# Scale half of the first modulation loaded ahead of the shift half, the low-rank shift added in PSUM, decay midpoints as the exponential's bias

## The reference

```python
sh1, sc1, ... = mod                       # mod = silu(cond) @ ada_w + ada_b, 6 x 1024 columns
h = rms_norm(x, pre_mix_g) * (1.0 + sc1) + sh1
proj = h @ w_in                           # conv value and gate, r, k, v
w_raw = w0 + tanh(h @ w1) @ w2            # decay, for each of two directions
w_log = -softplus(-w_raw) - 0.5
decay = exp(-exp(w_log))
a = sigmoid(a0 + (h @ a1) @ a2)
g = sigmoid(h @ g1) @ g2
```

## Time and profile before

| | us |
|---|---|
| median of 3 runs (lowest to highest) | 1207.55 (1206.76 to 1209.17) |
| the profiled execution's own time | 1206.84 |
| its span | 1205.0 |
| TensorE busy | 1123.2 (93%) |
| VectorE busy | 393.8 (33%) |
| ScalarE busy | 199.2 (17%) |

### The profile page before, as it was taken

One profiled execution on the slowest core, in us unless ns is written; L12 is line 12 of the kernel. 1 busy time (PEld: TensorE's weight loads), 2 busy tenths in 40 slices (PEclk: granted clock), 3 DMA queues, 4 the chain that ended last, 5 costly groups with the idle time before them and its releaser, 6 DMA issues.

```text
span 1205.0 us, 16442 instructions
## 1 busy us (share of the span) xinstructions
PE 1123.2 (93%) x6676; PEld 510.6 (42%) x6676; DVE 393.8 (33%) x935; ACT 199.2 (17%) x458; POOL 68.1 (6%) x113
## 2 busy tenths in 40 slices
PE   4999999999999999898999999999999898989997
PEld 2886776744434333333333333344333333333432
DVE  0598887654321212121212121213212121212123
ACT  2311344423111110101010101011111111110102
POOL 1003444400000000000000000000000000000000
PEclk9999999999999999999999999999999999999999
DMA  9900746888999999999999999999999999999995
GB/s 369 386 29 10 311 174 247 311 308 327 423 413 432 432 432 427 430 429 430 431 431 430 431 430 431 419 424 432 431 431 430 431 432 430 430 432 424 427 425 243
DMA packets 39948, 456.11 MB, mean 379 GB/s; under 512 B 5168, under 2 KB 5696, under 8 KB 16352
## 3 DMA queue, kind: packets, MB, share of 16 engines
q1 hardware_dynamic: 39112, 454.58, 90.0%
q0 software_dynamic: 480, 0.80, 0.2%
q10 hardware_dynamic: 312, 0.11, 0.0%
HBM read 454.13 MB, written 1.34 MB: 378 GB/s over the span
## 4 chain that ended last, share of the span: by engine, by line
PE 50%; DMA 44%; DVE 4%; issue 1%; ACT 1%; SPq 0%; DVEq 0%; ACTq 0%
DMA ring<-in_w_gu 39%; PE bank L637 24%; PE bank L675 5%; PE bank L757 5%; DMA front<-in_w_down 3%; DMA ring<-in_ada_w 2%; PE bank L1028 2%; PE bank L592 2%; PE bank L582 1%; PE bank L752 1%; PE bank L872 1%; PE bank L767 1%; PE bank L814 1%; PE bank L887 1%; PE bank L617 1%
## 5 line engine op out<-in xcount | busy, mean ns | idle before, releaser
L637 PE MATMUL bank<-ring,front 128*64 128x512 f32 x2032 | 461.3, 609 | 36.0 <-DMA ring<-in_w_gu 36.0
L637 PEld LDWEIGHTS bank<-ring,front 128*64 128x64 f32 x2032 | 143.9, 140 | 351.2 <-issue 283.8
L1521 DVE TENSOR_SCALAR front<-bank 128x512 f32<-128x512 f32 x32 | 22.1, 692 | 481.6 <-PE bank L637 481.6
L675 PE MATMUL bank<-front 128*64 128x512 f32 x512 | 113.6, 595 | 9.5 <-ACT front L1159 9.1
L675 PE MATMUL bank<-ring,front 128*64 128x512 f32 x512 | 113.4, 595 | 5.1 <-ACT front L1159 5.1
L1151 ACT ACTIVATE front<-front 128x512 f32<-128x512 f32 x32 | 20.2, 631 | 488.1 <-DVE front L1521 488.1
L1545 DVE COPY front<-bank 64x512 f32<-64x512 f32 x32 | 21.9, 683 | 175.1 <-PE bank L675 175.1
L675 PEld LDWEIGHTS bank<-front 128*64 128x64 f32 x512 | 36.3, 137 | 76.5 <-issue 73.3
L675 PEld LDWEIGHTS bank<-ring,front 128*64 128x64 f32 x512 | 36.3, 137 | 71.9 <-issue 70.4
L592 PE MATMUL bank<-front 128*128 128x512 f32 x136 | 62.9, 605 | 1.5 <-DVE front L1545 1.5
L582 PE MATMUL bank<-front 128*128 128x128 f32 x480 | 56.0, 275 | 0.0
(11 more groups left out here) (272 smaller groups left out, 901.6 us busy)
## 6 DMA issues: line engine op xcount, KB each, us to landing
ring<-in_w_gu SPq DMA_DIRECT2D x46, 4096.0 KB
front<-in_w_down SPq DMA_DIRECT2D x30, 2048.0 KB, 19.5
ring<-in_w_down SPq DMA_DIRECT2D x28, 2048.0 KB, 20.2
ring<-in_w_gu SPq DMA_DIRECT2D x25, 2048.0 KB
ring<-in_ada_w SPq DMA_DIRECT2D x24, 1024.0 KB, 11.7
ring<-in_w_gu SPq DMA_DIRECT2D x20, 1024.0 KB
ring<-in_w_in SPq DMA_DIRECT2D x5, 2048.0 KB, 19.9
ring<-in_w_down SPq DMA_DIRECT2D x6, 1024.0 KB, 10.1
```

The costliest lines, as they stand in the source:

```text
L637: last = pe.matmul(ps[r][64 * hf:64 * hf + 64, :], xT[:, k, S * q:S * q + S], rows, start=False, stop=(k == order[-1]))
L675: last = pe.matmul(ps[2][64 * c:64 * c + 64, :], actT[:, m, 64 * hf:64 * hf + 64], wdn[q][hf][:, m, c * 512:(c + 1) * 512], start=(k == 0) ...
L1521: v.tensor_scalar(glu, ps[0], 7.0, None, ALU.min).then_inc(s["glu_ready"], 1)
```

## The change

- The scale columns of `ada_w` are loaded first, in eight pieces of 512 KB; then `lora1`; then the shift columns, in four pieces of 1 MB that cover two k each. Their four semaphores are ones used later for something else, whose later waits are raised by 16.
- TensorE's order is: scale products of k = 0 to 3 (four column tiles of 256 columns now), the eight small transposes, k = 4 and 5, the transposes of x, k = 6 and 7, two turned blocks. ScalarE and VectorE write `hT` without the shift, and TensorE runs the first two low-rank products on it.
- Then, for each k, TensorE runs the four shift matmuls and one matmul of the third low-rank product. The shift is turned (two blocks) and lands in `shift_pad` (32 columns per k, two used, cleared by POOL). `shift_pad` times `lora1` (eight matmuls of 384 columns, four column tiles) is copied to `shift_l1`, and three matmuls against a 0/1 pattern add it to the three banks.
- `hT` is written again with scale and shift while this goes on; the projections wait for it, and items 4 to 7 wait because their banks hold x. The decay products wait for two `mids` in place of three.
- The third block of `w_in` waits for 16 counts of `ada0_acc` in place of 8.
- The sums in `Pc` keep their origin. VectorE writes plus and minus half of KAPPA times their last columns to `mid_log` (two small operations per q in place of eight), and ScalarE takes eight exponentials of 129 columns per head pair in place of two of 516, with `mid_log` as bias.

The core of the diff:

```diff
             for k in range(KC):
-                sp.dma_start(ada0[:, k, :], ada_w[k * P:(k + 1) * P, 0:2048]).then_inc(in_ada0[k], 16)
+                sp.dma_start(ada0[:, k, D:2 * D], ada_w[k * P:(k + 1) * P, D:2 * D]).then_inc(in_ada0[k], 16)
             for hf in range(2):
                 sp.dma_start(lora1[:, 4 * hf:4 * hf + 4, :], lora1_in[:, 4 * hf:4 * hf + 4, :])\
                     .then_inc(s["in_lora_b" if hf else "in_lora"], 16)
+            for k in range(0, KC, 2):
+                sp.dma_start(ada0[:, k:k + 2, 0:D], ada_w[k * P:(k + 2) * P, 0:D].rearrange("(k p) n -> p k n", p=P))\
+                    .then_inc(in_shift[k // 2], 16)
...
-                    sp.wait_ge(s["ada0_acc"], KC)
+                    sp.wait_ge(s["ada0_acc"], 2 * KC)
...
+            def first_rows_of(k, col):
+
+                for j in range(4):
+                    last = pe.matmul(ps[0][32 * j:32 * j + 32, 0:256], siluT[:, k, :],
+                                     ada0[:, k, col + j * 256:col + j * 256 + 256],
+                                     start=(k == 0), stop=(k == KC - 1), skip_group_check=True)
+                last.then_inc(s["ada0_acc"], 1)
...
+            pe.wait_ge(s["silu"], 1)
+            scale_rows(range(4))
...
+            scale_rows(range(4, 6))
             pe.wait_ge(s["xn"], 2)
...
+            scale_rows(range(6, KC))
             keep_clock(1)
             pe.wait_ge(s["mod0"], 1)
+            turn_first(0)
             keep_clock(1)
             for k in range(KC):
...
                 for n in range(2):
+                    pe.matmul(bank_of(n)[:, 0:N], lora1[:, k, n * P:(n + 1) * P], hT[:, k, :],
+                              start=(k == 0), stop=False, skip_group_check=True)
+            for k in range(KC):
+                if k % 2 == 0:
+                    pe.wait_ge(in_shift[k // 2], 16)
+                first_rows_of(k, 0)
+                pe.matmul(bank_of(2)[:, 0:N], lora1[:, k, 2 * P:3 * P], hT[:, k, :], start=(k == 0), stop=False,
+                          skip_group_check=True)
+            pe.wait_ge(s["mod0"], 2)
+            turn_first(256)
+            pe.wait_ge(s["modT"], 2)
+            for k in range(KC):
+                j = k % 4
+                last = pe.matmul(ps[0][32 * j:32 * j + 32, 0:3 * P], shift_pad[:, k, :], lora1[:, k, :],
+                                 start=(k < 4), stop=(k >= 4), skip_group_check=True)
+            last.then_inc(s["mod0_tr"], 1)
+            pe.wait_ge(s["in_rw"], 32)
+            pe.wait_ge(s["mod0"], 3)
+            for n in range(3):
+                pe.matmul(bank_of(n)[:, 0:N].rearrange("p (g t) -> p g t", g=G), shift_l1[:, n * P:(n + 1) * P],
+                          const[:, K_E2:K_E2 + G].unsqueeze(2).broadcast_to([P, G, T]), start=False, stop=True,
+                          skip_group_check=True).then_inc(s["l2_mm"], 1)
...
+                if 4 <= n < 8:
+
+                    rewritten = s["hT_a"] if n < 6 else s["hT_v"]
+                    pe.wait_ge(rewritten, KC + 4 * (n % 2 + 1))
...
-                    pe.wait_ge(s["a_sig"], 3)
+                    pe.wait_ge(s["a_sig"], 2)
...
                 for sg, sc in enumerate((-KAPPA, KAPPA)):
-                    last = a.activation(Ex[:, sg], Pc[:, :, r], ACT.Exp, scale=sc)
+                    for d in range(2):
+                        for g in range(G):
+                            last = a.activation(Ex[:, sg, d, g, :], Pc[:, d, r, g, :], ACT.Exp, scale=sc,
+                                                bias=mid_log[:, sg, r, d, g:g + 1])
...
+            po.memset(shift_pad, 0.0)
             po.memset(siluT, 0.0).then_inc(s["silu_pad"], 1)
...
+            v.wait_ge(s["ada0_acc"], 2 * KC)
+            v.tensor_copy(mod0[:, 256:512], ps[0][:, 0:256]).then_inc(s["mod0"], 1)
+            v.wait_ge(s["mod0_tr"], 2)
+            for m in range(2):
+                last = v.tensor_tensor(shift_pad[:, :, 0:G].rearrange("p (f h l) r -> p l f h r", f=2, h=2)[:, m], turned(m),
+                                       by_half(first_T[:, 0], m, 0), ALU.add)
+            last.then_inc(s["modT"], 1)
+            v.wait_ge(s["modT"], 2)
+            for c in range(KC):
+                hf, m = divmod(c, 4)
+                v.tensor_scalar(hT[:, c, T:N], ps[3 + c // 4][:, (c % 4) * T:(c % 4 + 1) * T],
+                                modT[:, m, 2 * (2 + hf) + 1:2 * (2 + hf) + 2], shift_pad[:, c, 1:2],
                                 ALU.mult, ALU.add).then_inc(s["hT_v"], 1)
+                if c == 3:
+                    v.wait_ge(s["mod0_tr"], 3)
+                    v.tensor_copy(shift_l1, ps[0][:, 0:3 * P]).then_inc(s["mod0"], 1)
...
-                        v.tensor_scalar(half, run[:, T:T + 1], 0.5, None, ALU.mult).then_inc(s["v_step"], v_at.mark("sgw_used"))
-                        v.wait_ge(s["v_step"], v_at.after("sgw_used", n + 1))
-                        v.tensor_scalar(run, run, half, None, ALU.subtract).then_inc(s["pre"], 1)
+                v.wait_ge(s["scan"], 4 * q + 4)
+                for sg, sc in enumerate((0.5 * KAPPA, -0.5 * KAPPA)):
+                    last = v.tensor_scalar(mid_log[:, sg, q], Pc[:, :, q, :, T], sc, None, ALU.mult)
+                last.then_inc(s["pre"], 1)
```

More of the change, by code:

```diff
@@ L158, in build @@
         modT = view(r_kb[:, 0:32], "p (m r) -> p m r", m=4)
-        mod0 = r_E[:, 0:512]
+        mod0, shift_l1 = r_E[:, 0:512], r_E[:, 512:896]
+        shift_pad = view(r_kb[:, 512:768], "p (k m) -> p k m", k=KC)
         first = view(r_ra[0:4 * G, 0:1024], "p (n c) -> p n c", n=2)
@@ L680, in _, with scale_rows, turn_first, keep_clock @@
         def _(pe):
-            pe.wait_ge(s["in_const"], 16)
+            def first_rows_of(k, col):
[4 more added lines that the diff above has]
+                last.then_inc(s["ada0_acc"], 1)
+            def scale_rows(ks):
+                for k in ks:
+                    pe.wait_ge(in_ada0[k], 16)
+                    first_rows_of(k, D)
+            def turn_first(col):
+                for m in range(2):
+                    last = pe.matmul(ps[0][:, m * 8:(m + 1) * 8], mod0[:, col + m * P:col + (m + 1) * P], used_rows,
+                                     start=True, stop=True)
+                last.then_inc(s["mod0_tr"], 1)
+            def keep_clock(count):
+                for _ in range(count):
+                    pe.matmul(ps[7], ident, xn[:, 0, 0:512], start=True, stop=True)
+            pe.wait_ge(s["in_const"], 16)
+            pe.wait_ge(s["silu"], 1)
+            scale_rows(range(4))
+            pe.wait_ge(s["in_mod"], 64)
+            for n in range(2):
+                for m in range(4):
+                    last = pe.matmul(ps[5][:, n * 32 + m * 8:n * 32 + m * 8 + 8], first[:, n, m * P:(m + 1) * P],
+                                     ident[0:4 * G, 0:4 * G], start=True, stop=True)
+            last.then_inc(s["first_tr"], 1)
+            scale_rows(range(4, 6))
             pe.wait_ge(s["xn"], 2)
@@ L687, in _ @@
                 last.then_inc(s["xT_tr"], 1)
[L688 to L705, removed]
+            scale_rows(range(6, KC))
             keep_clock(1)
             pe.wait_ge(s["mod0"], 1)
-            for m in range(4):
-                last = pe.matmul(ps[0][:, m * 8:(m + 1) * 8], mod0[:, m * P:(m + 1) * P], used_rows, start=True, stop=True)
-            last.then_inc(s["mod0_tr"], 1)
+            turn_first(0)
             keep_clock(1)
@@ L734, in _ @@
                         pe.wait_ge(s["kk"], emptied(n - 7, "v"))
[L735 to L739, removed]
+                if kind in "wa":
                     pe.wait_ge(s["in_lora2"], 48)
-                    pe.wait_ge(s["a_sig"], 3)
+                    pe.wait_ge(s["a_sig"], 2)
                     rows = slice(LORA * d, LORA * d + LORA)
@@ L1564, in _, with turned, by_half @@
                 .then_inc(s["v_step"], v_at.mark("first_one"))
+            def turned(m):
+                return ps[0][:, 8 * m:8 * m + 8].rearrange("p (f h r) -> p f h r", f=2, h=2)
+            def by_half(x, m, j0):
+                return x.rearrange("p (h l) j r -> p l j h r", l=2)[:, m, j0:j0 + 2]
             v.wait_ge(s["ada0_acc"], KC)
-            v.tensor_copy(mod0, ps[0]).then_inc(s["mod0"], 1)
+            v.tensor_copy(mod0[:, 0:256], ps[0][:, 0:256]).then_inc(s["mod0"], 1)
             v.wait_ge(s["mod0_tr"], 1)
             v.wait_ge(s["v_step"], v_at.after("first_one", 1))
-            v.tensor_tensor(modT.rearrange("p m r -> p (m r)"), ps[0][:, 0:32],
-                            first_T[:, 0].rearrange("p m j r -> p (m j r)"), ALU.add).then_inc(s["v_step"], v_at.mark("modT"))
+            modT4 = modT.rearrange("p m (j r) -> p m j r", r=G)
+            for m in range(2):
+                last = v.tensor_tensor(by_half(modT4, m, 2), turned(m), by_half(first_T[:, 0], m, 2), ALU.add)
+            last.then_inc(s["v_step"], v_at.mark("modT"))
             v.wait_ge(s["v_step"], v_at.after("modT", 1))
```

(4 more changed lines are left out.)

46 lines of the change are left out of this document (22 added, 24 removed).

## The result

The changed kernel takes 1213.52 us (1212.01 to 1213.66, 5 runs) against 1207.55: ratio 1.0049 (95% interval 1.0036 to 1.0061), 6.0 us. The profiled execution took 1213.52, span 1211.7, which is 6.7 us over that of before. The sign is the one forecast; the time is 2.5 us over the 1211 named, outside the forecast's own range (1209.5 to 1213) and just at the upper end of the wide one (1213.5).

What follows compares the result with a forecast made beforehand. Bound: first modulation's weight transfer to 27.83 us, TensorE to 118.47, mostly expert weights from about 407. Terms -7.7 + 0.0 + 9.8 - 3.5, plus chain 6.35 against 1.3, gave +3.7: 1211 us; own range 1209.5 to 1213, wide 1206.3 to 1213.5.

Steps and rivals of the forecast that it cites:

- Scale half first, last scale product at 21.5, low-rank work from 24.2: Front: loading scale columns first ends scale products 7.4 us sooner and starts low-rank work at 24.2 against 31.92.
- Mixed steps 1.23 us each, 9.8: Shift and third low-rank bank on TensorE: eight steps, 0.16 to 0.21 us lost per change of shape, 9.8 in all.
- No DMA wait after piece 3: Front: TensorE waits for no transfer after scale piece 3; the last shift pair lands near 31.8, wanted about 39.
- shift chain 6.35 with the table load exposed: Between mixed steps and decay sigmoids: new chain of 6.35 us against 1.3 before, including an unhidden 1.28 us sigmoid table load.
- Decay sigmoids to first projection 3.7: From first decay sigmoid to first wide projection: stays 3.7 us, set by ScalarE at 0.38 each.
- Midpoints and exponentials 0: Head pairs: VectorE's 4.7 us relief and ScalarE's 2.2 to 2.8 us of exponentials for 1.16 both count 0.
- the cover named: ScalarE around the tightest exponentials, at 181.17: idle 0.78 plus 0.72 us, to absorb an excess of 1.0 to 1.6.
- The sign given for B: Under 71 us from the first wide projection to the successor of the product at 118 would show the forecast wrong.
- B: Projections: VectorE was the hidden bound, so 4.7 us come back; 1203.6 with a front without shape-change loss; chance 0.16.
- A shift at 118 us moves the whole rest by as much: Expert transfers wait for buffers TensorE frees, so a TensorE shift at 118 us moves expert stage and end equally.
- Rival C: Front as forecast, exponentials late at three head pairs, first evictions meeting the rewrites: +3.7 + 2.0, 1213.2; chance 0.08.

Runs made afterwards that it cites:

- e2: The kernel before with only the decay midpoints and exponentials changed; 1207.50 us, ratio 1.0001.
- e3: The changed kernel with all 32 shift products first, then the eight of the third low-rank bank; 1210.12 us, ratio 1.0023.
- e7: The changed kernel with tanh made as 2 sigmoid(2x) - 1, so ScalarE needs one table; 1211.8 us, one run.
- e6: The changed kernel with pieces of the second modulation's weights held until 20 copies of the head pair are done; 1211.16 us, one run.
- e8: The changed kernel with filler, shift products in one run, third-bank products in the shift chain's gaps, one table and held loads; 1204.81 us, ratio 0.9973.
- e9: The changed kernel with filler, shift products in one run, third-bank products in the shift chain's gaps and one table, no held loads; 1205.16 us, ratio 0.9977.
- e4: The kernel before with 43 small filler products on TensorE ahead of its first transposes; 1207.45 us, ratio 1.0003.
- after_again: The changed kernel as it is, measured a second time; 1213.59 us, ratio 1.0048.
- e1: The changed kernel with the decay midpoints and exponentials of before, so only the front is changed; 1211.57 us, ratio 1.0035.
- e5: The changed kernel with five filler products of 128 columns behind the first four scale pieces; 1207.01 us, one run.
- e10: The changed kernel with five filler products behind the first four scale pieces, timed again; 1208.0 us, ratio 1.0009.

## Why the prediction was right in sign and short in size

- *Scale half first, last scale product at 21.5, low-rank work from 24.2.* Piece 3 came at 12.90 as forecast (12.8). The step failed at the 8 small transposes: 2.24 us in the earlier trace rows was itself a mean over two rates, since TensorE reached its full rate within them, at 16.2 us. In the changed order it reached it only at 21.7. So 3.58 for 2.24, 1.94 for 1.07, then 3.10 for 3.65: last scale product 23.4, low-rank work 25.88, **+1.7**. In the old order a slow stretch is hidden by the transfer: in e2 the full rate came only at 24.4, the small transposes took 3.58, and the first projection came at 47.45 all the same.
- *Mixed steps 1.23 us each, 9.8.* Right: 1.20 each, 9.6; e3 showed that the changes of shape are what costs.
- *No DMA wait after piece 3; shift chain 6.35 with the table load exposed.* Right: 42.61 to 48.86 is 6.25. e7 gave 0.8 of it back.
- *Decay sigmoids to first projection 3.7.* 3.77.
- *Midpoints and exponentials 0.* Right (e2), by the cover named. The sign given for B, less than 71 us from the first wide projection to 118's successor, could not have told: the stretch is 70.9 us in before and in after.
- *A shift at 118 us moves the whole rest by as much.* This step was wrong in its "as much". At the new timing a pause of 1.5 to 1.8 us stands at the end of the first head pair, right behind the transfers of the second modulation (DMA share 1.02 up to 137, 0.13 after); with the clock drop the loss is 2.9. No rival named it. Rival C had +2.0 more, about the right size, from two causes of which neither is seen; that the wide range, which takes its upper end from C, still reaches to the measured time is luck.

Sum: forecast 3.7 + 1.4 in the front (1.7 less 0.3 elsewhere) + 2.9 in the head pair - 1.2 in the rest = 6.7 of the profiled span, as rounded.

What stays open. Among the kernels with a changed front the pause is absent only where the loads were held (e6, e8); e9 has it with a front as early as before's. It is 0.3 to 0.6 us at first projections from 47.6 to 51.6, and 1.5 to 1.8 at 52.6 and later; but e3 had 1.8 at 49.44 and e4 0.7 at 52.76. e6, e8 and the packets above speak for an instruction load that comes late while those transfers run. They don't show whose instructions the packets hold, nor what in the front's timing makes a packet late. Nor is it settled why e8 and e9 end 2.4 and 2.0 us ahead of before, though their experts start no earlier. One profiled execution per kernel, e9's 2.6 us over its median, can't tell, with the scatter of the expert stage.

## What to carry to other kernels

A duration read while another engine or a transfer sets the end may hold a slow state of the engine that nobody paid for; before bringing such work onto the path, look at the same operation later in the trace and take both rates as bounds. When loaded data comes in earlier, count every change of shape, copy and table load that leaves the transfer's shadow with it: here they cost more than the earlier start gave. A shifted front also moves the transfers that follow it against the work beside them, here with a pause of up to 1.8 us, so "the rest moves by as much" needs a margin of its own.

## What was unexpected of the hardware

- TensorE's first work ran at the rate of its lower level (1.2 GHz) for a time that differed between executions. By the first clock record, the full rate came at 16.2 us in before and 24.4 in e2, which have the same work there, at 20.3 to 23.9 in the seven executions with the changed front and no filler, and at 11.4 to 14.3 in the five with filler. In e2 the engine had then worked without a wait for 12.4 us. The transposes of x took 3.10 in after, 3.68 in after_again, 3.60 in e1, 2.42 in e3, and 1.97 with filler (e5, e10; 2.52 and 3.00 in e8 and e9, where the clock fell again). Five products of 128 columns in the gaps were worth 0.40% of the kernel. The Trainium skill ("TensorE: Matmul & The Clock Gate", What's actually happening) says that an idle engine starts at the lower level and that the time at which it leaves it varies from run to run, by half a microsecond either way. These rows agree in kind, but vary by more: 3.6 us among those seven.
- The opposite in e4: brought early to the full rate, the engine fell to a granted 0.50 from 24.5 to 38.2 us, at first while it waited for pieces; that execution's front ended 5.2 us later. Filler in the gaps of after did not always prevent a fall either (e8, e9 above).
- A change between 32-column tiles and the full array cost 0.18 us on average over both directions, with no wait for data (e3).
- A pause of 0.3 to 1.8 us in TensorE's work with nothing that it waits for in the profile, 2.3 to 2.6 us from a packet of the instruction queue to the next product.
